# A two-layer encoder with routed experts on one Trainium2 core: the first item's rounds reordered around its gather in quarters, the router's product turned, and expert numbers read ahead

## The reference

```python
def hier_moe(h, w_rg, b_rg, w_re, b_re, w_gate, w_up, w_down):
    g_logits = xt @ w_rg + b_rg                      # 4 groups
    grp = argmax(g_logits); p_grp = softmax(g_logits)[grp]
    e_in = (xt @ w_re + b_re).reshape(n, 4, 8)[grp]  # 8 experts in the group
    top_v, top_i = lax.top_k(e_in, 2)
    gate = p_grp[:, None] * softmax(top_v)
    ...
    y = (silu(xb @ w_gate[e]) * (xb @ w_up[e])) @ w_down[e]
    ...
for l in range(2):
    x = x + mixer_sublayer(x, ...)
    x = x + hier_moe(rms_norm(x, norm2_g[l]), ...)
```

## Time and profile before

| | before |
|---|---|
| median of 3 runs | 1157.78 us (1156.81 to 1157.81) |
| the profiled execution | 1157.88 us, its span 1156.1 us |
| TensorE busy | 988.2 us (85%) |
| VectorE busy | 291.4 us (25%) |
| ScalarE busy | 178.2 us (15%) |
| transfers | 437.07 MB, mean 378 GB/s |
| mean granted TensorE clock | 0.929 of full |

### The profile page before, as it was taken

One profiled execution on the slowest core, in us unless ns is written; L12 is line 12 of the kernel. 1 busy time (PEld: TensorE's weight loads), 2 busy tenths in 40 slices (PEclk: granted clock), 3 DMA queues, 4 the chain that ended last, 5 costly groups with the idle time before them and its releaser, 6 DMA issues.

```text
span 1156.1 us, 13593 instructions
## 1 busy us (share of the span) xinstructions
PE 988.2 (85%) x5406; PEld 464.8 (40%) x5406; DVE 291.4 (25%) x794; ACT 178.2 (15%) x444; POOL 51.6 (4%) x104
## 2 busy tenths in 40 slices
PE   8999999998886955649999999999969889374687
PEld 5556654453342412113355656444534334131142
DVE  3556552111110110001145565421111101100011
ACT  1244311010010100001024343111100101000010
POOL 2121100000000000000021211000000000000000
PEclk9999999998997977878999999999999999787799
DMA  9962889999999999999998248899999999999997
GB/s 315 329 274 110 353 302 418 425 428 428 428 427 427 427 430 425 429 427 421 400 395 312 105 175 335 334 419 427 427 427 430 425 427 429 430 426 426 428 419 306
DMA packets 61878, 437.07 MB, mean 378 GB/s; under 512 B 10909, under 2 KB 15349, under 8 KB 31349
## 3 DMA queue, kind: packets, MB, share of 16 engines
q1 hardware_dynamic: 61813, 436.17, 91.8%
HBM read 435.10 MB, written 1.44 MB: 378 GB/s over the span
## 4 chain that ended last, share of the span: by engine, by line
PE 63%; DMA 31%; DVE 3%; SPq 1%; issue 1%; POOL 1%; ACT 0%; DVEq 0%; POOLq 0%
PE bank L1061 31%; DMA ring<-in_w_down 16%; DMA ring<-in_w_gate 10%; PE bank L770 9%; PE bank L1087 5%; DMA ring<-in_w_up 5%; PE bank L902 5%; PE bank L1015 4%; PE bank L729 2%; PE bank L848 1%; PE bank L838 1%; SPq L515 1%; PE bank L870 1%; PE bank L1079 1%; PE bank L861 1%
## 5 line engine op out<-in xcount | busy, mean ns | idle before, releaser
L1061 PE MATMUL bank<-ring,work 128*32 128x512 f32 (+2 forms) x2608 | 485.8, 669 | 133.0 <-DMA ring<-in_w_up 51.9
L1061 PEld LDWEIGHTS bank<-ring,work 128*32 128x32 f32 (+2 forms) x2608 | 147.0, 131 | 398.1 <-issue 396.3
L770 PE MATMUL bank<-ring,hT 128*128 128x512 f32 (+1 forms) x384 | 128.3, 488 | 1.2 <-DVE hT L1416 1.2
L770 PEld LDWEIGHTS bank<-ring,hT 128*128 128x128 f32 x384 | 71.4, 190 | 48.6 <-issue 42.4
L1015 PEld LDWEIGHTS bank<-work,h 128*128 128x128 f32 x704 | 82.3, 192 | 16.6 <-issue 15.7
L1015 PE MATMUL bank<-work,h 128*128 128x128 f32 x704 | 86.8, 278 | 1.7 <-DVE work L1777 1.7
L1061 PE MATMUL bank<-work 128*32 128x512 f32 (+2 forms) x176 | 74.9, 617 | 12.4 <-DMA ring<-in_w_down 12.4
L1087 PE MATMUL bank<-work 128*128 128x512 f32 x176 | 81.4, 604 | 2.4 <-ACT work L1369 1.6
L1061 PE MATMUL bank<-kept,work 128*32 128x512 f32 (+1 forms) x160 | 75.5, 626 | 5.8 <-DMA ring<-in_w_up 5.8
L1833 DVE COPY work<-bank 128x512 f32<-128x512 f32 x20 | 13.8, 692 | 242.5 <-PE bank L1061 242.5
L1828 DVE TENSOR_TENSOR work<-work,bank 128x512 f32<-128x512 f32 x22 | 15.1, 688 | 219.4 <-PE bank L1061 219.4
(11 more groups left out here) (209 smaller groups left out, 718.9 us busy)
## 6 DMA issues: line engine op xcount, KB each, us to landing
ring<-in_w_gate SPq DMA_DIRECT2D x42, 2048.0 KB, 25.6
ring<-in_w_down SPq DMA_DIRECT2D x38, 2048.0 KB, 23.9
ring<-in_w_up SPq DMA_DIRECT2D x36, 2048.0 KB, 29.6
ring<-in_w_up SPq DMA_DIRECT2D x36, 1024.0 KB, 14.8
ring<-in_w_down SPq DMA_DIRECT2D x28, 1024.0 KB, 10.2
ring<-in_w_gate SPq DMA_DIRECT2D x20, 1024.0 KB, 9.1
ring<-in_w_in SPq DMA_DIRECT2D x8, 1536.0 KB, 13.7
ring<-in_w_out SPq DMA_DIRECT2D x8, 1024.0 KB, 17.2
```

Of the source, the lines that this page charges most:

```text
L770: last = matmul(bank[6 + i % 2][:, 0:c1 - c0], hT[:, k, t * P:t * P + P], group_in(l, gi)[:, k, c0:c1], start=(k == 0), stop=(k == KD - 1))
L1061: last = nc.tensor.matmul(bank[b][e * w:e * w + w, :], lhs[:, k, e * w:e * w + w], rows(pos, k_count // 2)[:, kk, n * 512:n * 512 + 512], ...
```

## The change

It has four parts, and one small one.

1. **The router's product.** `logits` now holds w_route still (36 columns) and moves both tiles' hT (256 columns) in one product for each block; it waits for both tiles. The result lies as 36 rows x 256 columns. VectorE copies it to SBUF (`lgT`, in the room of `pick`), TensorE turns it back with two transposes. VectorE's `router` then handles both tiles in each step. Only one of the two match-and-replace steps stays in it; the other one and the marks oh1 and oh2 move to `choices`, ahead of the gates. Three warming calls instead of four follow.
2. **The first item.** Its gather goes by quarters into banks 0 to 3. Half of it (two quarters) stands before the rounds; then come gate0 and up0, the other half of the gather, gate1, the turning of pickw, and up1. VectorE copies quarters 0, 1 and 3 (`copy_quarter`), ScalarE quarter 2. The plan of the ring follows the new order (`FIRST_ORDER`): the first two pieces of item 2 take the slots of up0, the next two those of gate1.
3. **VectorE's order in `first`.** Copies of quarters 0 and 1 stand before the rest of the expert order; the copy of quarter 3 stands behind pickw and ahead of `seatings`.
4. **Expert numbers.** SyncE reads the four numbers of item 2 ahead of the last piece of item 1.
5. In the last item of layer 1, five warming calls follow round up1 instead of two.

```diff
-BESIDE_FREE = [("p_pv", 8, 24)] * 4 + [("p_logit", 2, 40), ("a_rows", TT, 41), ("p_pv", 8, 24)]
+BESIDE_FREE = [("p_pv", 8, 24)] * 4 + [("p_logit", 1, 40), ("a_rows", TT, 41), ("p_pv", 8, 24)]
...
+FIRST_ORDER = (0, 2, 1, 3, 4, 5)
...
-                done = ("p_down", 2 * q + 2) if r == 5 else ("p_round", 5 * q + r + 1)
+                n = FIRST_ORDER.index(r) if i == 0 else r
+                done = ("p_down", 2 * q + 2) if r == 5 else ("p_round", 5 * q + n + 1)
...
-                        take((l, i, r, e), 1, done, t0 + 100 + 10 * i + r, allowed)
+                        take((l, i, r, e), 1, done, t0 + 100 + 10 * i + n, allowed)
...
+        lgT = pick.rearrange("p t s -> p (t s)")[0:36]
...
+            def named(l, r):
+                return bass.ds(sp.value_load(order[0:1, r:r + 1], min_val=0, max_val=NE - 1), 1)
+            def ordered(l, i):
+                sp.wait_ge(v_order, 2 * l + 1 + (RANK0[TIME[i]] + KINDS[TIME[i]] > 16))
+                sp.sem_inc(seen[0], 1)
+            ahead = []
             def item(l, i, q):
                 r0 = RANK0[TIME[i]]
                 n = KINDS[TIME[i]]
-                if r0 >= NS:
-                    sp.wait_ge(v_order, 2 * l + 1 + (r0 + n > 16))
-                    sp.sem_inc(seen[0], 1)
                 ids = [bass.ds(e, 1) for e in STATIC[r0:r0 + n]] if r0 < NS else []
+                if i == 2:
+                    ids = ahead[4 * l:4 * l + n]
...
+                    ordered(l, i)
...
-                            ids.append(bass.ds(sp.value_load(order[0:1, r0 + e:r0 + e + 1], min_val=0, max_val=NE - 1), 1))
+                            ids.append(named(l, r0 + e))
+                        if i == 1 and (l, i, r, e) in HALVED:
+                            ordered(l, 2)
+                            ahead.extend(named(l, RANK0[TIME[2]] + f) for f in range(KINDS[TIME[2]]))
...
-            def logits(l, t):
-                pe.wait_ge(v_yT, 2 * l + t + 1)
-                pe.wait_ge(a_yT, 2 * l + t + 1)
+            def logits(l):
+                pe.wait_ge(v_yT, 2 * l + 2)
+                pe.wait_ge(a_yT, 2 * l + 2)
                 for k in range(KD):
-                    last = matmul(bank[4 + 2 * t][:, 0:36], hT[:, k, t * P:t * P + P],
-                                  w_route[:, k, :], start=(k == 0), stop=(k == KD - 1))
+                    last = matmul(bank[4][0:36, 0:SEQ], w_route[:, k, :], hT[:, k, :], start=(k == 0), stop=(k == KD - 1))
                 last.then_inc(p_logit, 1)
+                pe.wait_ge(v_logit, l + 1)
+                for t in range(TT):
+                    last = transpose(bank[6][:, t * 36:t * 36 + 36], lgT[:, t * P:t * P + P], ident[0:36, 0:36])
+                last.then_inc(p_route, 1)
...
-                logits(l, 0)
-                logits(l, 1)
-                warm(7, 4)
-                pe.wait_ge(v_chosen, 2 * l + 2)
+                logits(l)
+                warm(7, 3)
+                pe.wait_ge(v_chosen, l + 1)
...
+            def gather_first(half):
+                for n in (2 * half, 2 * half + 1):
+                    for k in range(2):
+                        for t in range(TT):
+                            last = matmul(bank[n][:, k * P:k * P + P], x_kc[:, t, 2 * n + k, :], pick[:, t, :],
+                                          start=(t == 0), stop=(t == TT - 1))
+                    last.then_inc(p_gather if n % 2 else p_first, 1)
             def first(l):
                 pe.wait_ge(a_rows, TT * (l + 1))
-                gather(0, l * NI)
+                pe.wait_ge(v_pick, l * NI + 1)
+                gather_first(0)
...
+                            if i == 0 and r < 2 and kk == 2:
+                                if r == 0:
+                                    pe.wait_ge(v_xg, q + 1)
+                                else:
+                                    pe.wait_ge(v_first, 2 * l + 2)
...
-                pe.wait_ge(v_xg, q + 1)
+                if i == 0:
+                    pe.wait_ge(v_first, 2 * l + 1)
+                else:
+                    pe.wait_ge(v_xg, q + 1)
                 round_of(0, (b0,), xg, p_round)
+                if i == 0:
+                    round_of(2, (b1,), xg, p_round)
+                    gather_first(1)
...
-                round_of(2, (b1,), xg, p_round)
+                if i:
+                    round_of(2, (b1,), xg, p_round)
...
-                    warm(b0, 2)
+                    warm(b0, 2 if l < LAYERS - 1 else 5)
...
-                gathered(0, l * NI)
+                act.wait_ge(p_first, 2 * l + 2)
+                for k in range(4, 6):
+                    last = nc.scalar.mul(xg[:, k, :], bank[2][:, (k - 4) * P:(k - 3) * P], gain2[:, l, k:k + 1])
+                last.then_inc(a_xg, 1)
...
-                act.wait_ge(p_round, 5 * q + 2)
+                act.wait_ge(p_round, 5 * q + (3 if i == 0 else 2))
...
-                router(l, 0)
-                router(l, 1)
-                gl, el = lg[:, :, 0:NG], lg[:, :, NG:36]
-                left = rb[:, :, 0:NE], ra[:, :, 0:NE]
-                tt(oh1, left[0], el, ALU.not_equal)
-                link(tt(oh2, left[1], left[0], ALU.not_equal))
+                router(l)
+                gl = lg[:, :, 0:NG]
...
+            def router(l):
+                dve.wait_ge(p_logit, l + 1)
+                nc.vector.tensor_copy(lgT, bank[4][0:36, 0:SEQ]).then_inc(v_logit, 1)
+                dve.wait_ge(p_route, l + 1)
                 dve.wait_ge(d_route, 64 * (l + 1))
-                dve.wait_ge(g_rstd, rooted(l, ("y0", "y1")[t]))
-                gl, el = lg[:, t, 0:NG], lg[:, t, NG:36]
-                link(stt(lg[:, t], bank[4 + 2 * t][:, 0:36], rstd[:, 2 + t:3 + t], b_route[:], ALU.mult, ALU.add))
-                link(nc.vector.tensor_reduce(col[:, 0, t:t + 1], gl, AX_X, ALU.max))
-                link(stt(ra[:, t, 4:8], gl, col[:, 0, t:t + 1], rev[:, 0:NG], ALU.is_equal, ALU.mult))
-                link(nc.vector.tensor_reduce(col[:, 1, t:t + 1], ra[:, t, 4:8], AX_X, ALU.max))
-                els = el.rearrange("p (g e) -> p g e", g=NG)
-                link(stt(els, wide(ra[:, t, 4:8], EPG), col[:, 1, t:t + 1], els, ALU.subtract, ALU.add))
-                link(nc.vector.max(top[:, t, :], el))
-                link(nc.vector.tensor_copy(firsts[:, :, t, 0], top[:, t, 0:2]))
-                left = rb[:, t, 0:NE], ra[:, t, 0:NE]
-                for c in range(2):
-                    link(nc.vector.match_replace(out=left[c], in_to_replace=firsts[:, c, t],
-                                                 in_values=(el, left[0])[c], imm_value=-3e38))
-                tt(chosen[:, t], left[1], el, ALU.not_equal).then_inc(v_chosen, 1)
+                dve.wait_ge(g_rstd, rooted(l, "y1"))
+                gl, el = lg[:, :, 0:NG], lg[:, :, NG:36]
+                for t in range(TT):
+                    last = stt(lg[:, t], bank[6][:, t * 36:t * 36 + 36], rstd[:, 2 + t:3 + t], b_route[:], ALU.mult, ALU.add)
+                link(last)
+                link(nc.vector.tensor_reduce(col[:, 0, :], gl, AX_X, ALU.max))
+                for t in range(TT):
+                    last = stt(ra[:, t, 4:8], gl[:, t], col[:, 0, t:t + 1], rev[:, 0:NG], ALU.is_equal, ALU.mult)
+                link(last)
+                link(nc.vector.tensor_reduce(col[:, 1, :], ra[:, :, 4:8], AX_X, ALU.max))
+                for t in range(TT):
+                    els = el[:, t].rearrange("p (g e) -> p g e", g=NG)
+                    last = stt(els, wide(ra[:, t, 4:8], EPG), col[:, 1, t:t + 1], els, ALU.subtract, ALU.add)
+                link(last)
+                for t in range(TT):
+                    last = nc.vector.max(top[:, t, :], el[:, t])
+                link(last)
+                link(nc.vector.tensor_copy(firsts[:, 1, :, 0:2], top[:, :, 0:2]))
+                for t in range(TT):
+                    last = nc.vector.match_replace(out=ra[:, t, 0:NE], in_to_replace=firsts[:, 1, t], in_values=el[:, t], imm_value=-3e38)
+                link(last)
+                tt(chosen[:], ra[:, :, 0:NE], el, ALU.not_equal).then_inc(v_chosen, 1)
...
+            def choices():
+                el = lg[:, :, NG:36]
+                link(nc.vector.tensor_copy(firsts[:, 0, :, 0], top[:, :, 0]))
+                for t in range(TT):
+                    last = nc.vector.match_replace(out=rb[:, t, 0:NE], in_to_replace=firsts[:, 0, t], in_values=el[:, t], imm_value=-3e38)
+                link(last)
+                tt(oh1, rb[:, :, 0:NE], el, ALU.not_equal)
+                link(tt(oh2, ra[:, :, 0:NE], rb[:, :, 0:NE], ALU.not_equal))
             def gates(l):
+                choices()
...
+            def copy_quarter(l, n, done):
+                tt(xg[:, 2 * n:2 * n + 2, :], bank[n][:, 0:2 * P].rearrange("p (k s) -> p k s", k=2),
+                   wide(gain2[:, l, 2 * n:2 * n + 2], P), ALU.mult).then_inc(done, 1)
...
+                dve.wait_ge(p_first, 2 * l + 1)
+                copy_quarter(l, 0, v_first)
```

(30 more changed lines are left out.)

## The result

The changed kernel takes 1161.93 us (median of 6 runs, 1161.53 to 1163.86) against 1157.72 us; the ratio is 1.0032 with a 95% interval of 1.0021 to 1.0043. It is slower by 4.2 us, where 3.6 us was forecast. The profiled execution took 1162.53 us, its span is 1160.7 us, 4.6 us over that of before.

What follows compares the result with a forecast made beforehand. The prediction took each layer's weight stream, nearly dry when item 1 begins, to bound the kernel. Layer 0's +2.3 us and layer 1's +1.3 made +3.6 on 1157.9, given as 1161.4 us, range 1157.6 to 1164.8.

Steps and rivals of the forecast that it cites:

- The product: Router, w_route held still: 16 instructions in 3.46 us, ending near 141.1 us, nothing saved.
- The chain: VectorE's joint router chain: 2.75 us for both tiles; with the product, the expert choice comes 1.8 us later.
- The gather by quarters: Item 0's gather cut into quarters: TensorE's sum stays the same, nothing gained, nothing lost.
- The new wait on VectorE: Behind quarter 3's copy: TensorE waits 1.1 us for item 1's pick and 0.4 us more before turning hidden values.
- TensorE at item 1: Item 1's first round: 3.3 us of delays less 0.2, so 3.1 us later in layer 0.
- What the stream absorbs: Weight transfers at item 1: 0.8 us of TensorE's lateness stays hidden in each layer, leaving +2.3 us in layer 0.
- rival of the router's delay alone: Without VectorE's late seatings: 1.8 - 0.8 = 1.0 us, nothing in layer 1, 1158.9 us; within a rival of chance 0.2.
- Layer 1's clock: Layer 1's warming matmuls before the ranks: 1.0 us lost at half clock is not paid again, leaving +1.3 us.
- Reading ahead and the last warming calls: Early expert numbers and three more calls in the last item (2.3 us at most, within a 3.11 us wait): nothing.
- the stream sets the end from its first release on: Rival: item 2's first four half pieces go out sooner, some 1.2 us gained for each layer, 1155.5 us; chance 0.15.
- One of the two delays isn't there: Rival: 1158.9 us without VectorE's late seatings, or 1158.6 us without the router's delay; chance 0.2.
- The clock falls: Rival: half clock under the first rounds, 1.7 us lost for each layer hit, 1163 to 1166 us; chance 0.15.

Runs made afterwards that it cites:

- e1: Kernel before with only the router's part of the change (turned product, both tiles in each VectorE step, three warming calls): 1161.76 us, ratio 1.0031.
- e6: Kernel before with one copy and one match-and-replace per tile in the router chain, oh1 and oh2 moved to the gates: 1157.28 us, ratio 0.9992.
- e5: Kernel before with three extra warming calls behind item 0's round up1 in each layer: 1160.19 us, ratio 1.0022.
- e2: Changed kernel with the old router (a product and a chain for each tile, four warming calls): 1159.01 us, ratio 1.0008.
- e4: Changed kernel with products for each tile as before, no copy or turning back, VectorE's chain still joint for both tiles: 1159.83 us, ratio 1.0015.
- e10: Kernel of e7 with three warming calls instead of four: 1155.82 us, ratio 0.9979.
- e8: Changed kernel with item 2's expert numbers read when needed and two warming calls instead of five at the end: 1162.75 us, ratio 1.0040.
- e7: Changed kernel with e6's router (products for each tile, four warming calls) and quarter 3 copied by ScalarE: 1156.09 us, ratio 0.9984.
- e3: Changed kernel with the copy of quarter 3 given to ScalarE instead of VectorE: 1160.73 us, ratio 1.0026.
- e9: Changed kernel with four warming calls behind the turned product instead of three: 1161.81 us, ratio 1.0035.

## Why the prediction was right, and where it was not

The time, 1161.4 us forecast and 1161.93 measured, came out by TensorE's two delays, which the rows show where they were forecast. The price of these delays is less well tested. The table takes, for each profile, when item 0's fifth and sixth rounds had ended (start of the first sum, L1087 before and L1131 in the changed kernel) and when the last transfer of the layer that the chain waits for had landed (the chain's start plus its length). The last two columns are the difference in layer 0 and in layer 1.

| kernel | rounds ended, layer 0 | last transfer, layer 0 | difference, layer 0 | difference, layer 1 |
|---|---|---|---|---|
| before | 174.12 | 572.72 | 398.60 | 396.55 |
| e1, router alone | 177.17 | 575.51 | 398.34 | 396.77 |
| e6, lean chain alone | 172.87 | 570.50 | 397.63 | 397.35 |
| e5, late delay | 175.82 | 573.30 | 397.48 | 398.40 |
| e2, order by quarters | 176.64 | 574.74 | 398.10 | 396.68 |
| e4, the same | 175.54 | 573.30 | 397.76 | 395.98 |
| e10, the same | 173.46 | 570.86 | 397.40 | 396.92 |
| changed, the same | 176.31 | 573.69 | 397.38 | 396.17 |
| e8, the same | 178.17 | 575.49 | 397.32 | 396.11 |
| e7, the same | 173.53 | 570.84 | 397.31 | 396.28 |
| e3, the same | 175.84 | 573.01 | 397.17 | 396.51 |
| e9, the same | 177.41 | 574.55 | 397.14 | 396.03 |

The row of the chain from which the changed kernel's landing comes:

```profile
555.56 18.13 DMA ring<-in_w_down
```

On how much is in hand the table gives only an estimate. The eight kernels with the order by quarters average 397.45 and 396.34 us, the three with the old order and no late delay (before, e1, e6) 398.19 and 396.89 us: 0.7 and 0.6 us of TensorE's lateness hidden, where 0.8 was forecast. But the values of one group scatter by up to 1 us, and two do not fit: e6 keeps the old order and lies near the others in layer 0, and e5, with its late delay, has the largest difference of all in layer 1.

The times say as much. Of a delay of 2 x 1.45 us, 0.8 us came through in e2; of 2 x 1.94 us, 2.2 in e5; of 2 x 1.96 us, 3.6 in e1. That something came through in e5 shows that the first releases, which e5 leaves alone, do not set the end by themselves. A delay that holds up the first releases as well, as in e1, seems to hide nothing, but the intervals of e1 and e5 overlap, so this is not shown.

Term by term, in the forecast's order:

- *The product.* Forecast 3.46 us for its 16 instructions, measured 3.62, tail included. The forecast choice of the row over the page was right: the Trainium skill's "TensorE: Matmul & The Clock Gate", section "Back-to-back issue gap", would give, as an estimate from its figure, 1.75 us.
- *The chain.* Forecast 2.75 us, measured 2.88. From first transpose to gather, +1.8 us was forecast and 1.96 measured. e4 gives the split, in part by an estimate: 2.1 us for the turned product, and 0.07 us back from the joint chain.
- *The gather by quarters.* "Nothing gained, nothing lost" was wrong by 0.35 us of TensorE's time in each layer (e3). TensorE's sum was not the same.
- *The new wait on VectorE.* Forecast 1.1 + 0.4 us; the idle shown is 0.60 + 0.16 us, and e3 gives 1.1 us for both with the restart of TensorE. With the 0.35 us above that makes 1.45 us against the forecast 1.5: the sum was right, its split not.
- *TensorE at item 1.* Forecast +3.1 us, measured 36.18 - 32.77 = 3.4.
- *What the stream absorbs.* Forecast 0.8 us in each layer. The pair before and changed gives 1.2 in layer 0 and 0.4 in layer 1, the averages above 0.7 and 0.6. The forecast's rival of the router's delay alone took the same 0.8 us off; there e1's 3.6 us (2.2 to 4.9) leave little room for it, since 3.9 less 1.6 would be 2.3.
- *Layer 1's clock.* The step that failed. The forecast gave back the 1.0 us that the fallen clock had cost before, as if it were a part of that kernel; the other profiles show it in some executions only. The forecast also said that the clock had fallen there behind a shorter idle stretch of TensorE, but it had been busy without a break from 708 to 716 us. In the changed kernel's profile that fall is gone, but the clock fell later, in the gather, and the fifth round came 1.6 us later than in layer 0 (37.78 against 36.18 us). Together layer 1 ended 1148.08 - 1143.45 = 4.63 us late, of which 0.97 came from layer 0. That layer 0 ended only 0.97 us late has a cause outside the change: its routed rows' first transpose came 1.23 us sooner (133.11 against 134.34 us). So the profiled pair agrees with the sum partly by two accidents. Layer 0 counted from its own first transpose, 573.69 - 133.11 = 440.58 us against 438.38, is +2.2 us where +2.3 was forecast, and that comparison is free of both. With the term left out, the forecast would have been 1162.4 us, as near to the median as 1161.4: it was luck that this mistake did not matter.
- *Reading ahead and the last warming calls.* Nothing, as forecast, as far as e8's one trace shows; its time leaves 0.7 us open.

Of the rivals, "the stream sets the end from its first release on" falls with e5. "One of the two delays isn't there" falls: e1's time shows the router's, e2's rows show the other, which is the smaller and by time not told from nothing. "The clock falls" happened in single executions; e9's profiled execution reaches the changed kernel's time without it.

## What to carry to other kernels

When a stream is held back at several points, ask which of them it reaches last with nothing in hand: time freed at an earlier one can merely move the idle stretch, as here to 173-176 us. A product turned to save instructions has to be counted in columns moved, and with the copy, the turning back and the overlap between tiles that it gives up. When a copy is moved behind a new wait, look at what stands behind it in the engine's order; given to an idle engine, the copy cost TensorE no wait (e3). And before a stretch of half clock in one profile is counted as a cost or a gain, look whether other executions show it.

## What the runs showed of the hardware that was not expected

The granted clock fell to half near the router in some executions and not in others, and at a different place for each form of the product. Of the 14 layers profiled with the small products (36 columns moving: before, e2, e4, e5, e6, e7, e10), 5 show it: in the last microsecond of the product (layer 1 of before, layer 0 of e4) or under the warming matmuls right behind it (e2, layer 1 of e4). With four calls it cost 1.0 us (the gather at 11.4 us instead of 10.4 in before and e2). TensorE had no idle before these falls: in layer 1 of before it was busy in all of each microsecond from 708 to 716 us. Of the 10 layers with the turned product (changed, e1, e3, e8, e9), 3 show it, all in the gather, some 6 us behind the product's end, where it cost 1.6 us. An estimate from these counts: with four calls behind the small products 3 of 10 layers fell, some 0.6 us for each execution, and with the turned product 3 of 10, some 1.0 us. So on average the change would give nothing back here.

The start of a run varies too. In the 12 profiles the first transpose of layer 0's routed rows lies between 133.11 us (changed) and 134.39 us (e2), though the change touches nothing of the mixers ahead of it. In the profile of before, ScalarE's wait for the second tile of x ended at 10.04 us and TensorE's projection went on at 11.61 us:

```profile
10.04 1.06 ACT L1194 ACTIVATE h<-x 128x1024 f32<-128x1024 f32 x1 [2.47 <-DMA x<-in_x]
11.61 0.67 PE L770 MATMUL bank<-ring,hT 128*128 128x256 f32 x2 [0.42 <-DVE hT L1416]
```

In that of the changed kernel the same happened at 8.77 and 10.40 us:

```profile
8.77 1.06 ACT L1245 ACTIVATE h<-x 128x1024 f32<-128x1024 f32 x1 [1.33 <-DMA x<-in_x]
10.40 1.94 PE L795 MATMUL bank<-ring,hT 128*128 128x256 f32 x8
```

This lead of 1.2 us was then kept through the whole of layer 0's mixers.
